# A hybrid decoder trunk on one core: the second stage with a Tanh for silu and inverse roots by Newton steps on GpSimd

## The chip, the cores and the metric

The kernel runs on one core of a Trainium2 chip. The metric is the device time of one execution in microseconds (us), the median of several runs. A core has five engines, each with its own instruction stream that it works off in order, and semaphores between them: TensorE (PE in the profile; its weight loads are listed as PEld), VectorE (DVE), ScalarE (ACT), GpSimd (POOL) and SyncE (SP), which here only issues DMAs.

## The reference, cut to what matters

The input is 2048 tokens of width 1024, ahead of which 16 "meta" tokens are set. Layer 0 is a gated DeltaNet with 8 heads of width 128: one projection to q, k, v and a gate z; a causal convolution of 4 taps and silu on q, k and v; k and q brought to unit length; then a chunked delta rule with a triangular system per chunk; a root-mean-square norm per head, times silu(z); an output projection. Layer 1 is sliding-window attention over a shared K/V, and a last norm follows. The change concerns layer 0 alone:

```python
def l2norm(x):
    return x * lax.rsqrt(jnp.sum(x * x, axis=-1, keepdims=True) + L2_EPS)

qkv = jax.nn.silu(causal_depthwise_conv(proj[..., :GDN_QKV_W], conv_w))
q = l2norm(qkv[..., :GDN_KEY_W].reshape(bsz, length, GDN_HEADS, GDN_DK)) * (GDN_DK ** -0.5)
k = l2norm(qkv[..., GDN_KEY_W:2 * GDN_KEY_W].reshape(bsz, length, GDN_HEADS, GDN_DK))
...
o = rmsnorm(o, o_norm) * jax.nn.silu(z.reshape(bsz, length, GDN_HEADS, GDN_DV))
```

## The kernel before

Four stages follow each other: norm and transposition of x, the DeltaNet (`gated_deltanet`, "second stage" here), its output projection with the shared K/V, and attention. The second stage works on 32 items: 4 groups of 512 tokens times 8 heads. The first 8 items (the head group) also carry a pass of their own for the 16 meta tokens, and in them the weights come in raw and are split in two parts (ScalarE rounds, GpSimd subtracts: `split_high`, `split_low`); later items load the parts.

An item goes through three steps of a pipeline, so step `it` has in hand item `it` (called p: projection, convolution, keys), item `it-1` (a: queries, the inverse of the triangular matrix X by levels) and item `it-2` (b: the scan over 4 chunks, norm, closing product). What lies where is written out by hand in `schedule`: 24 slots, each with its stages and with a number of projection matmuls (`FILL`) which TensorE works off after the slot's stages. Tables place the taps of the convolution (`TAPS`), the passes of the sigmoid (`SIGMOID`), silu (`SILU`), the copying of projections out of PSUM (`EVACUATE`), the splitting of weights (`SPLIT`) and the rows of the small triangular solve (`ROWS_P`, `ROWS_A`). Every engine runs through the same slots and does its own part; semaphores join them. Feature blocks are numbered f = 0 to 3 for k, v, q and z.

The lines that matter here, by the profile's numbers:

- L854 copies half a projection out of PSUM (ScalarE). L979 and L981 are the taps (VectorE), L983 a clamp at -40. L862, L865 and L868 are Exp, Ln and Exp of the sigmoid (ScalarE); L1002 and L1003 multiply silu out on VectorE, L1170 and L1171 on GpSimd (q and z in the head group).
- L1247 transposes kT (stage tokK, slot 12); L883 squares keys with a sum; L889, L894 and L895 (stage kk, slot 14) make 1/|k|^2 and |k| by Ln and Exp.
- L1050, L1052 and L1058 are VectorE's stage low (slot 15): the factors and the matrix nU. L1189 and L1194 are GpSimd's kg and qd, L1178 its part of splitting the weights, L843 ScalarE's.
- L1291, L1295 (left), L1308, L1311 (right), L1300 and L907 are the levels of the inverse (slots 13 to 18); between them VectorE writes half (L1083, L1087), X (L1095) and Xt (L1098).
- L1333 (ks), L1106 (r), L1342 (wr), L910 (w), L1347 and L1349 (out), L1111 (state) are the scan. L1116, L921, L922 and L926 are the output's norm, L1354 its transposes and L1125 the closing product (stage close, slot 16; slot 2 for a meta pass).
- L1023 and L1025 are the rows of the triangular solve.

Of the kernel before, what the change touches and what calls it, by code (L numbers as in the profile page):

```python
# [8 lines left out]
P = 128  # L9
# [3 lines left out]
META = 16  # L13
# [362 lines left out]
def gated_deltanet(nc, w_a, conv, o_gain, consts, table, xT_d, xg, oT_d, oTm_d, rows_d, rows_m_d, low_d, inv_d, w_d, w_out_next, w_raw):  # L376
# [6 lines left out]
    with nc.cleanup_on_exit(), ExitStack() as ctx:  # L383
# [18 lines left out]
        cst = sb("p2_cst", [P, 1])  # L402
# [8 lines left out]
        lnk = sb("p2_lnk", [P, 2, TPG])  # L411
# [28 lines left out]
        o_of = lambda p, c: ps_o1[:, P:2 * P] if p.meta else ps_o[c % 2][:, c * P:(c + 1) * P]  # L440
        ps_close = lambda p: ps_o1 if p.meta else ps_o0
# [20 lines left out]
        sig_done = sem("p2_sig_done")  # L462
# [8 lines left out]
        norm_ready = sem("p2_norm_ready")  # L471
        er_ready = sem("p2_er_ready")
# [35 lines left out]
        act_chain = sem("p2_act_chain")  # L508
# [28 lines left out]
        class Slot:  # L537
# [22 lines left out]
        def schedule(it, p, a, b, splitting):  # L560
# [17 lines left out]
            if b:  # L578
                if b[0].meta:
# [3 lines left out]
                    put(2, "close", b[0], 0)  # L583
                    put(4, "store", b[0], 0)
# [4 lines left out]
                put(16, "close", main, 0)  # L589
                put(18, "store", main, 0)  # L590
# [16 lines left out]
            if p:  # L607
# [6 lines left out]
                for q in p:  # L614
                    put(10, "gates", q, 0)
# [13 lines left out]
            for s, (back, f, parts) in SIGMOID.items():  # L629
                base[s].sigmoid += [(it - back, f, n) for n in parts if item[back]]  # L630
# [2061 lines left out]
```

## Time and profile before

| what | value |
| --- | --- |
| median of 3 runs | 2732.87 us (2731.5 to 2733.49) |
| the profiled execution | 2739.68 us |
| its span | 2737.9 us |
| busy: PE, DVE, ACT, POOL | 91%, 61%, 41%, 17% |
| second stage, first to last transposes of kT | 152.04 to 1493.14 us |
| mean granted TensorE clock | 0.961 |

The profile gives each instruction's start and duration, and for an engine's idle time what ended it. Overlapped matmuls make a busy TensorE look fuller than its peak. The span is the trace's own length; the execution's time is 1.8 us over it and 6.8 us over the median.

### The profile page before, as it was taken

How to read it: one execution, taken by the hardware profiler on the slowest of the kernel's cores; microseconds unless marked ns; L12 is line 12 of the kernel's file. 1: busy time of each engine (PE TensorE's matmuls, PEld its weight loads, DVE VectorE, ACT ScalarE, POOL GpSimd, SP SyncE). 2: the span in 40 equal slices, each digit the busy share in tenths (PEclk: the TensorE clock that was granted, in tenths of full speed). 3: DMA queues.
4: the chain of work that ended last, by engine and by line, in shares of the span. 5: the costliest groups of instructions: out<-in, count | busy, mean ns of one | idle time of the engine just before them, and what ended most of it. 6: DMA issues, size and time to landing. Idle time of an engine off the chain costs nothing. (4 is left out here: it accounts for less than half of the span.)

```text
span 2737.9 us, 46422 instructions
## 1 busy us (share of the span) xinstructions
PE 2485.1 (91%) x17193; PEld 2188.9 (80%) x17193; DVE 1672.3 (61%) x3906; ACT 1128.2 (41%) x3326; POOL 453.5 (17%) x341
## 2 busy tenths in 40 slices
PE   5468888899999999999999789999998999999997
PEld 4468777789998999999999558878886777777775
DVE  4357777777777777777777332233333667666764
ACT  4244554544444444444444244423332333333332
POOL 0033343310000000000000011200000333223331
PEclk9789999999999999999999589999999999999998
DMA  6664454544445444444453067743456322222221
GB/s 193 201 252 151 140 173 154 180 135 131 148 140 191 145 134 138 141 150 132 133 174 105 17 195 252 257 169 143 161 197 232 127 70 87 87 71 78 70 71 49
DMA packets 273665, 395.36 MB, mean 144 GB/s; under 512 B 79394, under 2 KB 187506, under 8 KB 273042
## 3 DMA queue, kind: packets, MB, share of 16 engines
q1 hardware_dynamic: 240642, 371.25, 40.5%
q10 hardware_dynamic: 32800, 21.17, 2.6%
q8 instruction: 136, 2.23, 0.3%
q14 instruction: 87, 0.71, 0.1%
HBM read 268.95 MB, written 123.95 MB: 144 GB/s over the span
## 5 line engine op out<-in xcount | busy, mean ns | idle before, releaser
L1229 PE MATMUL p_psp<-xg,p_whi 128*128 128x264 f32 x4096 | 842.6, 295 | 27.5 <-POOL p_wlo L1178 17.4
L1229 PEld LDWEIGHTS p_psp<-xg,p_whi 128*128 128x128 f32 x4096 | 655.1, 191 | 31.8 <-issue 29.4
L1229 PE MATMUL p_psp<-xg,p_wlo 128*128 128x264 f32 x2048 | 606.1, 296 | 0.0
L1229 PEld LDWEIGHTS p_psp<-xg,p_wlo 128*128 128x128 f32 x2048 | 391.5, 191 | 0.0
L981 DVE SCALAR_TENSOR_TENSOR p_acc<-p_proj,p_taps,p_acc 128x528 f32<-128x528 f32 x288 | 244.8, 850 | 4.6
L1854 PE MATMUL first_q<-first_w,p_o 128*128 128x512 f32 (+1 forms) x864 | 208.3, 400 | 15.7 <-DVE first_w L1818 15.7
L1854 PEld LDWEIGHTS first_q<-first_w,p_o 128*128 128x128 f32 (+1 forms) x864 | 157.1, 184 | 60.2 <-issue 16.0
L2400 PE MATMUL first_q<-first_w,p_hT 128*128 128x512 f32 x720 | 193.5, 408 | 11.6 <-DMA p_hT<-hT_dram 11.3
L2400 PE MATMUL p_pso<-p_wo,p_oT 128*128 128x512 f32 x768 | 193.9, 403 | 7.9 <-DVE p_oT L2311 4.2
L862 ACT ACTIVATE p_sig<-p_sig 128x528 f32<-128x528 f32 x128 | 82.6, 645 | 282.2 <-DVE p_sig L983 282.2
L1854 PE MATMUL p_psz<-p_wk,p_o 128*128 128x512 f32 x768 | 181.3, 392 | 0.0
L2400 PEld LDWEIGHTS p_pso<-p_wo,p_oT 128*128 128x128 f32 x768 | 143.6, 192 | 43.2 <-issue 10.4
L1023 DVE TENSOR_TENSOR p_prod<-p_Xb,p_blk 32x4 f32<-32x4 f32 (+13 forms) x448 | 163.8, 366 | 6.8
L1854 PEld LDWEIGHTS p_psz<-p_wk,p_o 128*128 128x128 f32 x768 | 142.9, 188 | 29.1
L2400 PEld LDWEIGHTS first_q<-first_w,p_hT 128*128 128x128 f32 x720 | 128.3, 189 | 46.3 <-DMA p_hT<-hT_dram 11.7
L1178 POOL TENSOR_TENSOR p_wlo<-raw,p_whi 128x512 fp32r<-128x512 f32 x72 | 106.3, 1486 | 274.4 <-ACT p_whi L843 274.2
L2151 ACT ACTIVATE p_logits<-p_logits,p_top 128x144 f32<-128x144 f32 x256 | 102.7, 403 | 81.5 <-DVE p_top L2253 81.5
L1189 POOL TENSOR_TENSOR p_kg<-p_kT,p_er 128x512 f32<-128x512 f32 (+1 forms) x40 | 45.2, 1129 | 543.3 <-ACT p_er L879 542.9
L2380 POOL TENSOR_TENSOR p_swapped<-p_q,p_cs 128x256 f32<-128x256 f32 x31 | 36.9, 1191 | 583.1 <-DVE p_q L2272 374.9
L854 ACT ACTIVATE p_proj<-p_psp 128x264 f32<-128x264 f32 x256 | 98.8, 386 | 62.7 <-PE p_psp L1229 62.5
L1194 POOL TENSOR_TENSOR p_qd<-p_qT,p_er 128x512 f32<-128x512 f32 (+1 forms) x40 | 50.7, 1275 | 429.2 <-DVE p_qT L1003 429.2
L907 ACT ACTIVATE p_Xt<-p_pst 128x512 f32<-128x512 f32 x64 | 38.3, 598 | 186.7 <-PE p_pst L1300 186.7
(264 smaller groups left out, 4711.5 us busy)
## 6 DMA issues: line engine op xcount, KB each, us to landing
p_whi<-w_dram SPq DMA_DIRECT2D x92, 512.0 KB, 3.9
p_wlo<-w_dram SPq DMA_DIRECT2D x92, 512.0 KB, 4.9
raw<-w_a_in SPq DMA_DIRECT2D x36, 512.0 KB, 6.8
w_dram<-p_whi SPq DMA_DIRECT2D x34, 512.0 KB, 4.4
w_dram<-p_wlo SPq DMA_DIRECT2D x34, 512.0 KB, 5.3
p_o<-hT_dram SPq DMA_DIRECT2D x34, 512.0 KB, 4.8
hT_dram<-p_hT SPq DMA_DIRECT2D x32, 512.0 KB, 3.4
p_hT<-hT_dram SPq DMA_DIRECT2D x30, 512.0 KB, 4.4
```

Source lines behind the costliest of these rows:

```text
L854: nc.scalar.activation(proj[:, f % 2, 3 + half_ * HALF:3 + (half_ + 1) * HALF], ps_p[half_][:, 0:HALF], ACT.Copy).then_inc(proj_read, 1)
L862: ins = nc.scalar.activation(v, v, ACT.Exp, scale=-1.0)
L907: nc.scalar.activation(Xt[p.par][:, 0:TPG, :], chunks(ps_t), ACT.Copy).then_inc(xt_ready, 1)
L981: nc.vector.scalar_tensor_tensor(a, p[:, part:part + GW], w, a, ALU.mult, ALU.add).then_inc(tap_done, 1)
L1023: link(nc.vector.tensor_tensor(t3, x3[:, 0:i, 0:i].rearrange("p j c -> p c j"), b3[:, 0:i, i].unsqueeze(1).to_broadcast([rows, i, i]), ALU ...
L1178: nc.gpsimd.tensor_tensor(w_lo[:, f, cols], w_raw[:, f % 2, cols], w_hi[:, f, cols].bitcast(f32), ALU.subtract).then_inc(lo_ready, 1)
L1189: nc.gpsimd.tensor_tensor(kg[p.par][:, at, :], cols(kT), e_r[:, at, :], ALU.mult).then_inc(keys_grown, 1)
L1194: nc.gpsimd.tensor_tensor(qd[p.par][:, at, :], cols(qT), e_r[:, at, :], ALU.mult).then_inc(queries_grown, 1)
L1229: ins = nc.tensor.matmul(ps_p[half_][:, 0:HALF], (w_hi, w_lo)[i][:, f, kc * P:(kc + 1) * P], xg[:, g % 2, j, kc, half_ * HALF:(half_ + 1) ...
L1854: last = nc.tensor.matmul(out, stationary[i][:, kc, 0:rows], moving(j, kc), start=kc == 0 and n == 0, stop=kc == KC - 1 and n == 2)
L2151: last_ = nc.scalar.activation(logits[:, s_, :], logits[:, s_, :], ACT.Exp, bias=top[:, s_:s_ + 1], accum_out=den[:, s_:s_ + 1])
L2400: ins = nc.tensor.matmul(banks[b][:], stationary[i][:, kc, :], weights[j][:, kc, b * FB:(b + 1) * FB], start=kc == 0 and n == 0, stop=kc = ...
```

## The change

1. silu(x) becomes (tanh(x/2) + 1) * x, which is twice silu. One Tanh on ScalarE replaces Exp, Ln and Exp, the clamp goes, and VectorE multiplies in one operation for all f (GpSimd's part goes). The factors of 2 are taken out later (0.25 on the sums of squares, half the output gain). The activation table is the one that has Exp and Tanh.
2. 1/|k|^2 comes from VectorE's reciprocal in stage low; |k| and the output's 1/sqrt come from GpSimd: a seed by integer arithmetic on VectorE, then three Newton steps of four small operations, each waiting for the one before it (stages root_k in slot 18; root_o in slot 16, and slot 1 for a meta pass). Two small buffers, `root[:, 0]` and `root[:, 1]`, hold minus half, the value and a temporary.
3. The output's scaling, transposes, closing product and store move: from slots 12, 16 and 18 to 18, 20 and 22, for a meta pass from 0, 2 and 4 to 4, 6 and 8. Meta outputs and their transposes lie in ps_t, the bank of the inverse's transposes, instead of ps_o1; a TensorE wait in ks goes, and two others come.

```diff
+TANH_EXP = "exp_and_others"
+ROOT_SEED = 0x5F3759DF
+ROOT_STEPS = 3
...
-        o_of = lambda p, c: ps_o1[:, P:2 * P] if p.meta else ps_o[c % 2][:, c * P:(c + 1) * P]
-        ps_close = lambda p: ps_o1 if p.meta else ps_o0
+        o_of = lambda p, c: ps_t[:, 0:P] if p.meta else ps_o[c % 2][:, c * P:(c + 1) * P]
+        ps_close = lambda p: ps_t[:, P:2 * P] if p.meta else ps_o0
...
-        SILU = {11: (0, 0), 21: (0, 1), 0: (1, 2), 5: (1, 3)}
+        TANH = {9: (0, 0), 19: (0, 1), 22: (0, 2), 1: (1, 3)}
+        SILU = {10: (0, 0), 20: (0, 1), 23: (0, 2), 3: (1, 3)}
...
-                    put(2, "close", b[0], 0)
-                    put(4, "store", b[0], 0)
+                    put(1, "root_o", b[0], 0)
+                    put(4, "scale", b[0], 0)
+                    put(6, "close", b[0], 0)
+                    put(8, "store", b[0], 0)
...
-                put(16, "close", main, 0)
-                put(18, "store", main, 0)
+                put(20, "close", main, 0)
+                put(22, "store", main, 0)
...
+                for q in p:
+                    put(18, "root_k", q, 0)
...
+                put(16, "root_o", b[-1], 0)
+                put(18, "scale", b[-1], 0)
...
-                elif stage == "kk":
-                    l = lnk[:, p.which, 0:n]
-                    act.wait_ge(k_squared, k + 1)
-                    link(nc.scalar.activation(l, ssq[:, p.which, 0, 0:n], ACT.Ln, bias=cst[:]))
...
-                    nc.scalar.activation(rn2[:, p.which, 0:n], l, ACT.Exp, scale=-1.0).then_inc(norm_ready, 1)
-                    nc.scalar.activation(norm[:, p.which, 0:n], l, ACT.Exp, scale=0.5).then_inc(norm_ready, 1)
...
                 elif stage == "low":
+                    squared = n2[:, p.which, 0:n]
                     nc.vector.tensor_copy(e_last[par][:, p.which, 0:n], mine[:, 4, 0:n])
-                    dve.wait_ge(norm_ready, 2 * k + 1)
-                    nc.vector.scalar_tensor_tensor(nD[par][:, p.which, 0:n], rn2[:, p.which, 0:n], -1.0,
+                    link(nc.vector.tensor_scalar(squared, ssq[:, p.which, 0, 0:n], 0.25, L2_EPS, ALU.mult, ALU.add))
+                    link(nc.vector.reciprocal(rn2[:, p.which, 0:n], squared))
+                    nc.vector.scalar_tensor_tensor(nD[par][:, p.which, 0:n], rn2[:, p.which, 0:n], -0.25,
...
                     last.then_inc(low_ready, 1)
+                    if not zero(k):
+                        dve.wait_ge(norm_ready, k)
+                    if not zero(p.first):
+                        dve.wait_ge(vs_ready, p.first)
+                    link(nc.vector.tensor_scalar(root[:, 0, 0, 0:n], squared, -0.5, None, ALU.mult))
+                    nc.vector.tensor_scalar(root[:, 0, 1, 0:n].bitcast(i32), squared.bitcast(i32), -0.5, float(ROOT_SEED),
+                                            ALU.mult, ALU.add).then_inc(norm_seeded, 1)
...
+            def inverse_root(kind, n, last=None):
+
+                minus_half, y, t = (root[:, kind, x, 0:n] for x in range(3))
+                for turn in range(ROOT_STEPS):
+                    link(nc.gpsimd.tensor_tensor(t, y, y, ALU.mult))
+                    link(nc.gpsimd.tensor_tensor(t, t, minus_half, ALU.mult))
+                    link(nc.gpsimd.tensor_scalar(t, t, 1.5, None, ALU.add))
+                    step_done = nc.gpsimd.tensor_tensor(y, y, t, ALU.mult)
...
+                elif stage == "root_k":
+                    pool.wait_ge(norm_seeded, k + 1)
+                    y = inverse_root(0, p.n)
+                    nc.gpsimd.tensor_tensor(norm[:, p.which, 0:p.n], n2[:, p.which, 0:p.n], y, ALU.mult).then_inc(norm_ready, 1)
+                elif stage == "root_o":
+                    pool.wait_ge(ms_seeded, k + 1)
+                    inverse_root(1, p.n, last=ms_ready)
...
-                        if index == 1 and p.with_meta:
-                            pe.wait_ge(o_g_ready, k)
```

In the instruction lists, VectorE's stage low of the main pass in a head item reads as follows before the change (p_rn is rn2, p_psl the bank of the inverse's products, p_cur the pass's decays; a semaphore whose name begins with p1_ is one of this stage that has taken over a number of the first):

```order
L1050 COPY p_elast<-p_cur 128x4
L1052 SCALAR_TENSOR_TENSOR p_nD<-p_rn,p_cur 128x4 [waits p2_norm_ready]
L1058 SCALAR_TENSOR_TENSOR p_nU<-p_psc,p_nD,p_eg 128x128 [waits p2_decay_ready,p2_kk_ps,p2_scaled]
L1058 SCALAR_TENSOR_TENSOR p_nU<-p_psc,p_nD,p_eg 128x128 x3
L1125 SCALAR_TENSOR_TENSOR p_og<-p_pso,p_gain,p_zT 128x512 [waits p2_stored,p1_a_exp,p2_oT_ps]
L1095 TENSOR_TENSOR p_X<-p_X,p_psl 128x8x32 [waits p2_right_ps]
```

And with the change (p_n is n2, the sum of squares):

```order
L1034 COPY p_elast<-p_cur 128x4
L1035 TENSOR_SCALAR p_n<-p_ssq 128x4
L1036 RECIPROCAL p_rn<-p_n 128x4 [waits p2_dve_chain]
L1037 SCALAR_TENSOR_TENSOR p_nD<-p_rn,p_cur 128x4 [waits p2_dve_chain]
L1043 SCALAR_TENSOR_TENSOR p_nU<-p_psc,p_nD,p_eg 128x128 [waits p2_decay_ready,p2_kk_ps,p2_scaled]
L1043 SCALAR_TENSOR_TENSOR p_nU<-p_psc,p_nD,p_eg 128x128 x3
L1051 TENSOR_SCALAR p_root<-p_n 128x4 [waits p2_vs_ready,p2_norm_ready]
L1052 TENSOR_SCALAR p_root<-p_n 128x4 [waits p2_dve_chain]
L1087 TENSOR_TENSOR p_X<-p_X,p_psl 128x8x32 [waits p2_right_ps]
```

The closing product has left this place, four small operations have come, and the wait on norm_ready stands behind nU, ahead of the addition into X.

GpSimd in a head item before the change, from the kg products on (p_wlo are the weights' low parts):

```order
L1189 TENSOR_TENSOR p_kg<-p_kT,p_er 128x128 [waits p2_ks_ps,p1_a_exp,p2_er_ready]
L1189 TENSOR_TENSOR p_kg<-p_kT,p_er 128x512 [waits p1_a_exp,p2_er_ready]
L1178 TENSOR_TENSOR p_wlo<-raw,p_whi 128x512 [waits p1_cum_read] x4
L1170 TENSOR_TENSOR p_qT<-p_acc,p_sig 128x16 [waits p2_kq_ps,p2_queries_grown,p1_a_exp,p1_raw_in]
L1171 TENSOR_TENSOR p_qT<-p_acc,p_sig 128x512
```

And with the change, up to the first turn of the output's root:

```order
L1184 TENSOR_TENSOR p_kg<-p_kT,p_er 128x128 [waits p2_ks_ps,p1_a_exp,p2_er_ready]
L1184 TENSOR_TENSOR p_kg<-p_kT,p_er 128x512 [waits p1_a_exp,p2_er_ready]
L1173 TENSOR_TENSOR p_wlo<-raw,p_whi 128x512 [waits p1_cum_read] x2
L1159 TENSOR_TENSOR p_root<-p_root 128x4 [waits p2_ms_seeded]
L1160 TENSOR_TENSOR p_root<-p_root 128x4 [waits p2_pool_chain]
L1161 TENSOR_SCALAR p_root<-p_root 128x4 [waits p2_pool_chain]
L1162 TENSOR_TENSOR p_root<-p_root 128x4 [waits p2_pool_chain]
```

These four rows come three times; then the root of the meta key (128x1, with L1188 at its end, which signals norm_ready), then that of the main key (128x4). Only after these 38 steps come the other two of the four subtractions.

VectorE behind the inverse, from the row that gives the state's first value, with the change:

```order
L1068 MEMSET p_state 128x128
L1120 SCALAR_TENSOR_TENSOR p_og<-p_pso,p_gain,p_zT 128x512 [waits p2_stored,p1_a_exp,p2_oT_ps]
L984 SCALAR_TENSOR_TENSOR p_vT<-p_sig,p_acc 128x16 [waits p2_v_ps,p1_raw_in]
L986 SCALAR_TENSOR_TENSOR p_vT<-p_sig,p_acc 128x512
L961 TENSOR_SCALAR p_acc<-p_proj,p_taps 128x528 [waits p1_a_exp,p1_rows_ready]
L964 SCALAR_TENSOR_TENSOR p_acc<-p_proj,p_taps,p_acc 128x528 [waits p1_act_chain]
```

The closing product (L1120) and silu of v now stand ahead of the taps of q; before, the taps and the first rows of the solve stood ahead of silu of v.

## Rows read from the trace of the kernel before

**Rows 1.** The page, part 1: busy us, share of the span and count by engine.
```profile
PE 2485.1 (91%) x17193; PEld 2188.9 (80%) x17193; DVE 1672.3 (61%) x3906; ACT 1128.2 (41%) x3326; POOL 453.5 (17%) x341
```

**Rows 2.** Timeline of TensorE: start us, us, line, instruction [idle before, released by]; slot 12.
```profile
152.04 0.47 PE L1247 MATMUL p_psk<-p_ident,p_kT 128*128 128x128 f32 x1 [9.23 <-DVE p_kT L1003]
...
200.00 0.33 PE L1247 MATMUL p_psk<-p_ident,p_kT 128*128 128x128 f32 x1 [4.11 <-DVE p_kT L1003]
...
353.24 0.33 PE L1247 MATMUL p_psk<-p_ident,p_kT 128*128 128x128 f32 x1 [0.34 <-DVE p_kT L1003]
...
643.14 0.66 PE L1247 MATMUL p_psk<-p_ident,p_kT 128*128 128x128 f32 x4 [0.53 <-DVE p_kT L1003]
```

**Rows 3.** Stretches: an ordinary and a head item: us, busy by engine, clock, DMA, GB/s.
```profile
643.14:683.32 40.18, 38.92 (x321) 37.55 (x321) 30.66 (x86) 18.80 (x61) 2.56 (x2) 1.00 0.45 143
353.24:403.97 50.73, 42.49 (x338) 39.84 (x338) 37.82 (x97) 26.05 (x85) 19.24 (x16) 1.00 0.49 163
```

**Rows 4.** Timeline of TensorE, the ordinary item: its wait for the state.
```profile
669.10 0.49 PE L1333 MATMUL p_psc<-p_state,p_kg 128*128 128x128 f32 x2 [0.38 <-DVE p_state L1111]
```

**Rows 5.** Timeline of TensorE, the head item from 353.24: its waits over one us.
```profile
377.34 0.46 PE L1342 MATMUL p_psc<-p_r,p_Xt 128*128 128x128 f32 x2 [1.81 <-DVE p_r L1106]
...
387.70 0.48 PE L1229 MATMUL p_psp<-xg,p_whi 128*128 128x264 f32 x2 [1.03 <-ACT p_proj L854]
...
401.95 0.49 PE L1347 MATMUL p_psc<-p_w,p_kdec 128*128 128x128 f32 x2 [1.12 <-ACT p_w L910]
```

**Rows 6.** Timeline of VectorE, the same item, slots 15 to 21.
```profile
361.80 1.13 DVE L1058 SCALAR_TENSOR_TENSOR p_nU<-p_psc,p_nD,p_eg 128x128 f32<-128x128 f32 x4
362.84 0.74 DVE L1125 SCALAR_TENSOR_TENSOR p_og<-p_pso,p_gain,p_zT 128x512 f32<-128x512 f32 x1
363.50 0.41 DVE L1095 TENSOR_TENSOR p_X<-p_X,p_psl 128x256 f32<-128x256 f32 x1
...
368.28 0.41 DVE L983 TENSOR_SCALAR p_sig<-p_acc 128x528 f32<-128x528 f32 x1
...
370.81 0.18 DVE L1002 TENSOR_TENSOR p_vT<-p_acc,p_sig 128x16 f32<-128x16 f32 x1 [0.49 <-ACT p_sig L868]
370.90 0.69 DVE L1003 TENSOR_TENSOR p_vT<-p_acc,p_sig 128x512 f32<-128x512 f32 x1
```

**Rows 7.** Timeline of GpSimd, the same item: the subtraction of slot 15.
```profile
362.71 1.28 POOL L1178 TENSOR_TENSOR p_wlo<-raw,p_whi 128x512 fp32r<-128x512 f32 x1 [1.04 <-ACT p_whi L843]
```

**Rows 8.** Timeline of ScalarE, the same item, slot 15.
```profile
361.73 0.39 ACT L854 ACTIVATE p_proj<-p_psp 128x264 f32<-128x264 f32 x1
362.00 0.63 ACT L843 ACTIVATE p_whi<-raw 128x512 fp32r<-128x512 f32 x1
```

**Rows 9.** Groups of instructions of GpSimd, shapes apart: count | busy us, mean ns | idle before.
```profile
L1189 POOL TENSOR_TENSOR p_kg<-p_kT,p_er 128x128 f32<-128x128 f32 x8 | 3.7, 460 | 67.1 <-ACT p_er L879 67.1
L1170 POOL TENSOR_TENSOR p_zT<-p_proj,p_sig 128x16 f32<-128x16 f32 x7 | 1.5, 218 | 49.3 <-ACT p_sig L868 49.3
L2678 POOL MEMSET const-bfloat16-1.0<- 128x1 bf16 x1 | 0.1, 101 | 0.0
```

**Rows 10.** The same view: an operation (attention stage) that waits for GpSimd's operation before.
```profile
L2384 POOL TENSOR_TENSOR p_q<-p_q,p_cs 128x512 f32<-128x512 f32 x31 | 40.4, 1303 | 2.4
```

**Rows 11.** Groups of instructions of ScalarE: the second pass of the sigmoid.
```profile
L865 ACT ACTIVATE p_sig<-p_sig 128x528 f32<-128x528 f32 x128 | 82.9, 648 | 1.3
```

**Rows 12.** Stretches after TensorE's idle time, columns as above: the clock is third from last.
```profile
200.00:204.00 4.00, 4.00 (x21) 4.00 (x22) 0.86 (x4) 1.85 (x12) 0.00 (x0) 0.57 0.97 386
...
888.20:897.30 9.10, 8.70 (x47) 8.49 (x48) 3.69 (x11) 1.01 (x5) 1.28 (x1) 0.62 0.76 228
```

**Rows 13.** Timeline of TensorE, an ordinary item: the output's four transposes (slot 16).
```profile
851.12 0.60 PE L1354 MATMUL p_pso<-p_ident,p_on 128*128 128x128 f32 x4
```

**Rows 14.** Timeline of VectorE and of GpSimd, the head item: two operations at once.
```profile
387.82 1.12 DVE L1023 TENSOR_TENSOR p_prod<-p_Xb,p_blk 40x169 f32<-40x169 f32 x1
...
387.53 1.09 POOL L1171 TENSOR_TENSOR p_zT<-p_proj,p_sig 128x512 f32<-128x512 f32 x1
```

More of the change, by code:

```diff
@@ L410, in gated_deltanet @@
         ssq = sb("p2_ssq", [P, 2, 2, TPG])
-        lnk = sb("p2_lnk", [P, 2, TPG])
+        n2 = sb("p2_n2", [P, 2, TPG])
+        root = sb("p2_root", [P, 2, 3, TPG])
         norm = sb("p2_norm", [P, 2, TPG])
@@ L628, in schedule @@
                 base[s].taps += [(it - back, f, n) for n in parts if item[back]]
-            for s, (back, f, parts) in SIGMOID.items():
-                base[s].sigmoid += [(it - back, f, n) for n in parts if item[back]]
+            for s, (back, f) in TANH.items():
+                base[s].tanh += [(it - back, f)] if item[back] else []
             for s, (back, f) in SILU.items():
@@ L942, in step @@
                         evacuate(item, u)
-                    for item, f, part in slot.sigmoid:
-                        sigmoid(item, f, part)
+                    for item, f in slot.tanh:
+                        half_angle_tanh(item, f)
                     for item, f, part in slot.split:
                         split_high(item, f, part)
-            nc.scalar.preload_act_table_set(LN_EXP)
+            nc.scalar.preload_act_table_set(TANH_EXP)
             act.wait_ge(const_in, 16 * N_CONST)
@@ L966, in convolve @@
             def convolve(it, f, part):
-                p, a, v = proj[:, f % 2, :], acc[:, f % 2, :], sig[:, f % 2, :]
-                w = taps[:, 4 * f + part:4 * f + part + 1] if part < 4 else None
-                if part == 0 or f == 3:
+                p, a = proj[:, f % 2, :], acc[:, f % 2, :]
+                w = taps[:, 4 * f + part:4 * f + part + 1]
+                if part == 0:
                     dve.wait_ge(proj_read, 2 * NF * it + (2 * f + 2))
@@ L1134, in step @@
                     for q, item, f in slot.silu:
-                        if f < 2 or not splitting[1]:
-                            silu(q, item, f, b)
+                        silu(q, item, f, b)
                     for item, f, part in slot.taps:
@@ L1140, in step @@
                         solve_row(q, i)
-            nc.vector.memset(cst[:], L2_EPS)
             nc.vector.memset(proj[:, :, 0:3], 0.0)
@@ L1148, in _ @@
             dve.wait_ge(const_in, 16 * N_CONST)
+            link(nc.vector.tensor_scalar(gain[:], gain[:], 0.5, None, ALU.mult))
             dve.wait_ge(zeroed, 32)
@@ L1200, in step @@
                         stage_of(stage, q, index, b)
-                    for q, item, f in slot.silu:
-                        if f >= 2 and splitting[1]:
-                            silu(q, item, f, b)
                     for item, f, part in slot.split:
@@ L1298, in stage_of @@
                     if index:
+                        if index == 1 and b and b[0].meta:
+                            pe.wait_ge(o_g_ready, b[0].number + 1)
                         for c in range(n):
@@ L1320, in stage_of @@
                         pe.wait_ge(qk_ready, k + 1)
+                        if p.meta and a and a[0].meta:
+                            pe.wait_ge(vs_ready, a[0].number + 1)
                         if p.leading:
```

125 lines of the change are left out of this document (51 added, 74 removed).

## Prediction, made before the change was run

> **What bounds the kernel now.** I began with the page's busy times: TensorE is at work 91% of the span [rows 1], so a change pays only where TensorE waits. The diff stays inside the second stage, so I then listed TensorE's starts of one instruction that comes once a pass, the transposes of kT that open slot 12 [rows 2]. They divide the stage into items, and the table of stretches gives an item's length and TensorE's busy time in it [rows 3]: 38.92 us of 40.18 in an ordinary item, but 42.49 of 50.73 in one of the head group (items 0 to 7, each with its meta pass). An ordinary item can therefore give at most 1.26 us (24 items: 30 us) and a head item 8.24 us (8 items: 66 us). More can't be won, since TensorE's instructions stay what they are; what can be lost has no such limit.
>
> The waits say what the change can reach. In the ordinary item the larger two are 0.53 us for kT and 0.38 for the state [rows 2, 4]. In the head item the reader should see two kinds [rows 5]: ScalarE is late (1.03 us for a copied projection, 1.12 us for w) because it stands in the three passes of the old sigmoid, and VectorE is late (1.81 us for r).
>
> **The one place that decides: a wait put on VectorE.** The change keeps the seeds of all key roots in one small buffer, root[:, 0]. So before it writes the seeds of a pass, stage "low" waits until the root of the pass before is finished (norm_ready of at least k). In an ordinary item that was done long before. In a head item the pass before is the meta pass of the same item, and GpSimd computes that root only in slot 18, behind the two kg products, two subtractions of weights (slots 14 and 15) and, from item 2 on, the output's root (slot 16). VectorE comes to the wait in slot 15 and works strictly in order: the addition into X (L1095), on which TensorE's next step of the inverse (L1295) waits, stands right behind it.
>
> Worked out on the head item from 353.24: VectorE ends the products of "low" at 362.93 [rows 6]. GpSimd's second subtraction starts at 362.71, released by ScalarE, and takes 1.28 us: GpSimd is free at 363.99 [rows 7]. That moment stays, since ScalarE's copy at 362.00, on which it waits, stands behind the copy of a projection at 361.73, which TensorE sets [rows 8]. Then come 12 chained steps of the output's root and 13 of the meta key's.
>
> A chained GpSimd step of 1 or 4 columns has no row. The nearest are 0.218 us at 16 columns and 0.460 at 128, so 2.2 ns a column over about 0.19 [rows 9]; and where a GpSimd operation waits for the one before it, the idle time is 2.4 us over 31, 0.08 us each [rows 10]. I take 0.27 us. Bounds: 0.10 (a memset of one column, without a hand-over) and 0.54 (128 columns with it).
>
> 25 steps of 0.27 are 6.75 us: GpSimd is done at 370.74. Two small VectorE operations (0.18 each, as the 16-column one) and the addition of 0.41 follow: X is there at 371.51 instead of 363.91 [rows 6]. **TensorE stands 7.6 us longer per head item**, six times (items 2 to 7): 45.6 us. With 0.10 it would be 3.4 us, with 0.54 14.4. Item 1 has no output behind it, 12 steps less: 4.3 us. In item 0 no inverse is open, so TensorE waits for no X: 0. Sum **+50 us**.
>
> **The other terms.**
> - VectorE's crowded part, from slot 20 to slot 12, gets the closing product of the output (0.66 us until the next start) and, from GpSimd, silu of q (0.18 + 0.69, as vT's now), and loses two clamps of 0.41 [rows 6]: 0.7 us more before the first r, which is late already. With 0.3 for the moved transposes it is 1.0. GpSimd's root of the meta output falls beside later rows of the inverse: 0. Seven items: **+7 us**.
> - ScalarE loses two of three sigmoid passes, each 0.65 us [rows 11], four times an item. In head items this frees the waits of 1.03 and 1.12 us, of which I give 0.55 back to VectorE, the next one late. Seven times 1.6: **-11 us**. In ordinary items these passes lie beside TensorE's projections, which don't wait for them: 0.
> - TensorE's clock. After 4.11 us of idle time [rows 2] the next 4.00 us ran at a granted 0.57; one stretch of 9.10 us after another wait ran at 0.62 [rows 12]. Most of these is 1.2 instead of 2.4 GHz, worth 4.00 x 0.43 = 1.7 and 9.10 x 0.38 = 3.5 us. The new stall of 7.6 us, and the one before r, will do this too: 3 us in six items, **+18 us** (bounds 0 and 7 each).
> - Ordinary items. silu of k ends a slot earlier: -0.53. The closing transposes leave slot 16 for 20, so TensorE is there sooner at L1295; but X is not, for "low" gets four small operations (0.18 each) before the addition and loses only the 0.66 of the closing product [rows 6]: +0.4. Before the first r VectorE is some 1.1 us later (closing product and silu of q, less a clamp), TensorE only by the transposes (0.60 [rows 13]): +0.5 against the 0.38 that the state costs there today. Together 0 (bounds -0.9 and +0.5), 24 times: **0**. GpSimd's 25 steps lie between slots 14 and 20, beside a VectorE that mostly reads PSUM: 0; without that cover up to 0.2 us a step.
> - Start and end. Silu of k in items 0 and 1, for which TensorE waits 9.23 and 4.11 us [rows 2], is two ScalarE passes and a clamp shorter: -3 us. At the very end nothing hides the output's root, 12 x 0.27: +3 us. Together **0**.
> - SP's queue and the other stages move only with these shifts. The meta outputs' new bank takes away a TensorE wait on o_g_ready that shows no idle time in [rows 5]: 0.
>
> Sum: 50 + 7 - 11 + 18 = **+64 us**. The profiled execution took 2739.68 us, 1.8 over its span and 6.8 over the median of the three runs. Set on the median, the forecast is 2732.87 + 64 = **2797 us**.
>
> **A rule weighed.** A VectorE product with both operands in SBUF does not run beside a GpSimd operation here: started at 387.82, it ended at 388.94, 0.32 us after GpSimd's at 387.53 + 1.09 [rows 14]. The Trainium skill ("SBUF — State Buffer", section "SBUF: two separate sides") says that the two engines share one pair of ports as an exclusive lock, and that whoever comes second waits for the whole of the other's instruction. By that rule small work moved to GpSimd slows VectorE down; the trace agrees. My sum holds it at 0, for VectorE stands still during most of the new steps; the first rival prices it.
>
> **Rivals.**
> 1. *The lock decides* (0.10). Of the 50 GpSimd steps of a head item, the 25 that are not run while VectorE is held meet its rows and taps and hold it up by 0.2 us each [rows 9, 14]. For it: VectorE is the late engine in the crowded part, and the main key's root runs there. Against it: by my times most of that root is done before. 25 x 0.2 = 5 us in 7 items: 2797 + 35 = 2832 us.
> 2. *Faster: the shortened engines win* (0.07). Place: the two waits for ScalarE and that for kT in a head item (1.03, 1.12, 0.34 [rows 2, 5]) and the two in an ordinary one (0.53, 0.38). All gone, and no block: 7 x 2.5 + 24 x 0.9 = 39 us, 2694 us. It decides only if GpSimd has the meta root done when VectorE arrives, at 362.9; but the second subtraction starts only then, and 25 steps follow. Even at 0.10 us a step it comes 3.6 us too late.
> 3. *No change* (0.03). The block costs 3.4 us in six items and 2.1 in the seventh (0.10 a step), no clock falls, and ordinary items gain 0.9: 22 + 7 - 11 - 22 = -4 us, 2729 us.
>
> **How the numbers follow.** The forecast has 0.80. Its own bounds: at 0.10 us a step the block is 28 us less, the clock perhaps 8 less, ordinary items 10 less: 2751 us. At 0.54 it is 44 us more: 2841 us. The range 2751 to 2841 takes in rival 1 and leaves out rivals 2 and 3 and the forecast's tails. Differences under 0.2% (5.5 us) can't be told from none by a measurement of this kernel. Slower: the forecast and rival 1, 0.90; same 0.03; faster 0.07.
>
> **What would show it.** In a head item VectorE idle for 7 to 9 us, released by GpSimd, before the two small writes into p_root that follow the four products into p_nU; TensorE idle as long before the half-width step of the inverse, its clock lower right after; head items of 58 to 63 us. GpSimd's steps 0.25 to 0.3 us apart. TensorE's waits for a copied projection and for w gone there. Ordinary items of 39.3 to 40.8 us, without a wait for kT. The forecast is wrong if that idle time of VectorE is under 3 us, if the steps are far from 0.27 us, or if ordinary items move by over 1 us.

## The result and the profile after

The changed kernel takes **2809.05 us** (median of 4 runs, 2806.42 to 2815.97) against 2733.18 us of the kernel before in the same series: ratio 1.0266, 95% interval [1.0253, 1.0279], slower. The forecast was 2797 us (2751 to 2841). The profiled execution took 2806.55 us (span 2804.8), 66.9 us more than the profiled one before. That difference is what the traces can explain; the medians differ by 76 us because the execution profiled before lay 6.8 us above the median it was shown with, and the one after 2.5 below its own.

The page, part 1, busy us by engine, answers [rows 1]: ScalarE lost about a sixth of its work, GpSimd got 972 more instructions, TensorE has the same number and is busy 21.9 us longer.

```profile
PE 2507.0 (89%) x17193; PEld 2216.3 (79%) x17193; DVE 1666.6 (59%) x4046; ACT 953.0 (34%) x2870; POOL 684.7 (24%) x1313
```

Stretches of an ordinary and of a head item, to be held against [rows 3] (kT's transposes are L1248 now; these are later in the span, but the same kinds of item):

```profile
795.91:835.47 39.56, 38.71 (x323) 37.53 (x322) 30.32 (x87) 13.64 (x49) 9.58 (x27) 1.00 0.45 141
380.71:442.70 61.99, 46.80 (x338) 44.30 (x339) 39.09 (x110) 19.80 (x67) 26.32 (x62) 0.86 0.38 129
```

The ordinary item is 0.62 us shorter, the head item 11.26 us longer: 6.95 of it idle time of TensorE, and 4.31 us in which its 338 matmuls simply took longer, at a mean granted clock of 0.86.

TensorE in the head item, its waits over 0.3 us from the start to the scan (those of before are [rows 2, 5] and the two rows behind these):

```profile
380.71 0.33 PE L1248 MATMUL p_psk<-p_ident,p_kT 128*128 128x128 f32 x1 [0.87 <-DVE p_kT L986]
...
399.06 1.33 PE L1296 MATMUL p_psl<-p_X,p_nU 64*128 64x64 f32 x5 [8.02 <-DVE p_X L1087]
...
407.86 0.33 PE L1267 MATMUL p_pst<-p_ident,p_vT 128*128 128x128 f32 x1 [0.30 <-DVE p_vT L986]
...
413.01 0.46 PE L1336 MATMUL p_psc<-p_state,p_kg 128*128 128x128 f32 x2 [2.19 <-DVE p_vs L1057]
...
416.12 0.77 PE L1345 MATMUL p_psc<-p_r,p_Xt 128*128 128x128 f32 x2 [1.94 <-DVE p_r L1098]
```

And two rows of TensorE in the head item of the kernel before. The wait of 1.54 us for v belongs to the waits over one us, but [rows 5] and the prediction leave it out.

```profile
363.96 1.10 PE L1295 MATMUL p_psl<-p_X,p_nU 64*128 64x64 f32 x8 [0.33 <-DVE p_X L1095]
...
371.64 0.33 PE L1266 MATMUL p_pst<-p_ident,p_vT 128*128 128x128 f32 x1 [1.54 <-DVE p_vT L1003]
```

Of the 8.02 us for X all but 0.33 is new. So is the wait for the meta v (p_vs), which the text of the prediction did not name. VectorE at the same place: its products into nU end at 390.45, then it stands until GpSimd's L1188 has written the meta norm; the addition into X is third in line.

```profile
389.26 1.19 DVE L1043 SCALAR_TENSOR_TENSOR p_nU<-p_psc,p_nD,p_eg 128x128 f32<-128x128 f32 x4
398.31 0.17 DVE L1051 TENSOR_SCALAR p_root<-p_n 128x4 f32<-128x4 f32 x1 [7.86 <-POOL p_norm L1188]
398.52 0.17 DVE L1052 TENSOR_SCALAR p_root<-p_n 128x4 int32<-128x4 int32 x1
398.60 0.41 DVE L1087 TENSOR_TENSOR p_X<-p_X,p_psl 128x256 f32<-128x256 f32 x1
```

And GpSimd: the second subtraction, the first of 12 steps for the output, the first of 13 for the meta key, and the last.

```profile
390.16 1.28 POOL L1173 TENSOR_TENSOR p_wlo<-raw,p_whi 128x512 fp32r<-128x512 f32 x1 [2.41 <-ACT p_whi L846]
391.39 0.20 POOL L1159 TENSOR_TENSOR p_root<-p_root 128x4 f32<-128x4 f32 x1
...
394.73 0.19 POOL L1159 TENSOR_TENSOR p_root<-p_root 128x1 f32<-128x1 f32 x1
...
398.09 0.19 POOL L1188 TENSOR_TENSOR p_norm<-p_n,p_root 128x1 f32<-128x1 f32 x1
```

From 391.39 to 398.28 are 25 chained steps: 0.276 us each. Finally the clock at and behind the two pauses, third column from the end (1.00 is 2.4 GHz, 0.50 is 1.2 GHz); in [rows 3] the whole item ran at 1.00:

```profile
396.71:400.71 4.00, 1.65 (x8) 1.65 (x8) 1.34 (x4) 0.00 (x0) 2.69 (x12) 0.50 0.80 280
400.71:404.71 4.00, 4.00 (x23) 3.53 (x23) 1.10 (x3) 1.91 (x6) 1.64 (x8) 0.56 0.00 0
412.71:416.71 4.00, 1.76 (x11) 1.60 (x12) 2.92 (x9) 0.44 (x1) 1.28 (x1) 0.72 0.37 148
416.71:420.71 4.00, 4.00 (x20) 4.00 (x20) 1.49 (x8) 1.02 (x4) 0.71 (x4) 0.50 0.72 249
```

Taken over the second stage, from one start of the transposes to the next: items 2 to 7 together 65.8 us longer (306.72 to 372.52), item 1 5.55, item 8 3.06, items 9 to 30 together 7.7 shorter, start and end +0.2. That is the 66.9 us.

### The profile page after: what moved, and what is told of

The parts are those of the page before. It is cut to its first block and busy times, and to the rows that moved or that the text cites. A ratio compares the mean times of both kernels' runs of the same rounds, so it can differ in the third digit from the quotient of the medians.

```text
span 2804.8 us, 47209 instructions
## 1 busy us (share of the span) xinstructions
PE 2507.0 (89%) x17193; PEld 2216.3 (79%) x17193; DVE 1666.6 (59%) x4046; ACT 953.0 (34%) x2870; POOL 684.7 (24%) x1313
## 5 line engine op out<-in xcount | busy, mean ns | idle before, releaser
L1230 PE MATMUL p_psp<-xg,p_whi 128*128 128x264 f32 x4096 | 859.3, 299 | 20.6 <-POOL p_wlo L1173 17.4
L1230 PEld LDWEIGHTS p_psp<-xg,p_whi 128*128 128x128 f32 x4096 | 667.7, 195 | 24.1 <-issue 21.4
L1230 PE MATMUL p_psp<-xg,p_wlo 128*128 128x264 f32 x2048 | 613.6, 300 | 0.0
L1230 PEld LDWEIGHTS p_psp<-xg,p_wlo 128*128 128x128 f32 x2048 | 397.6, 194 | 0.0
L1006 DVE TENSOR_TENSOR p_prod<-p_Xb,p_blk 32x4 f32<-32x4 f32 (+13 forms) x448 | 150.8, 337 | 7.6
L902 ACT ACTIVATE p_w<-p_psc,p_nD 128x128 f32<-128x128 f32 x136 | 50.0, 367 | 198.5 <-PE p_psc L1345 197.8
L1008 DVE TENSOR_REDUCE p_Xb<-p_prod 32x2 f32<-32x4 f32 (+13 forms) x448 | 105.0, 234 | 15.4
```

The costliest lines, as they stand in the source:

```text
L902: nc.scalar.activation(w_sb[:], ps_c[:, P:2 * P], ACT.Copy, scale=nD[p.par][:, p.which, index:index + 1]).then_inc(w_ready, 1)
L1006: link(nc.vector.tensor_tensor(t3, x3[:, 0:i, 0:i].rearrange("p j c -> p c j"), b3[:, 0:i, i].unsqueeze(1).to_broadcast([rows, i, i]), ALU ...
L1008: link(nc.vector.tensor_reduce(x3[:, i, 0:i], t3, mybir.AxisListType.X, ALU.add))
L1230: ins = nc.tensor.matmul(ps_p[half_][:, 0:HALF], (w_hi, w_lo)[i][:, f, kc * P:(kc + 1) * P], xg[:, g % 2, j, kc, half_ * HALF:(half_ + 1) ...
```

## The experiments

Every run is set against runs of the kernel before on the same chip in the same series; their medians stood at 2733 to 2739 us. "Head" is the mean of items 2 to 7, "ordinary" one undisturbed item of the main group, both from the starts of kT's transposes.

| run | median us | ratio to before, 95% | head | ordinary |
| --- | --- | --- | --- | --- |
| before | | 1 | 51.1 | 40.18 |
| the change | 2809.05 | 1.0266 [1.0253, 1.0279] | 62.1 | 39.56 |
| two_sets | 2756.97 | 1.0078 [1.0061, 1.0094] | 54.4 | 39.57 |
| steps5 | 2844.25 | 1.0392 [1.0374, 1.0409] | 67.0 | 39.55 |
| vs_early | 2808.13 | 1.0259 [1.0241, 1.0276] | 62.2 | 39.57 |
| two_sets_vs | 2756.51 | 1.0066 [1.0049, 1.0083] | 54.6 | 39.57 |
| meta_root_early | 2764.59 | 1.0088 [1.0070, 1.0105] | 55.9 | 39.57 |
| two_sets_q0 | 2742.21 | 1.0002 [0.9985, 1.0020] | 54.4 | 39.26 |
| early_q0 | 2752.07 | 1.0054 [1.0038, 1.0071] | 54.3 | 39.31 |
| early_q0_steps2 | 2742.69 | 1.0016 [1.0007, 1.0026] | 53.4 | 39.27 |
| all_moves | 2734.41 | 0.9985 [0.9976, 0.9994] | 53.9 | 39.00 |
| all_moves_steps2 | 2715.08 | 0.9915 [0.9899, 0.9931] | 50.6 | 39.00 |
| k_silu11 | 2812.83 | 1.0273 [1.0257, 1.0289] | 62.1 | 39.62 |
| root_slot15 | 2732.24 | 0.9974 [0.9962, 0.9986] | 53.5 | 38.99 |

**Is it the shared buffer? (two_sets)** The two keys' roots get a buffer each, and the wait goes back to the item before.

```diff
-        root = sb("p2_root", [P, 2, 3, TPG])
+        root = sb("p2_root", [P, 3, 3, TPG])
...
-                    if not zero(k):
-                        dve.wait_ge(norm_ready, k)
                     if not zero(p.first):
+                        dve.wait_ge(norm_ready, p.first)
                         dve.wait_ge(vs_ready, p.first)
-                    link(nc.vector.tensor_scalar(root[:, 0, 0, 0:n], squared, -0.5, None, ALU.mult))
+                    link(nc.vector.tensor_scalar(root[:, p.which, 0, 0:n], squared, -0.5, None, ALU.mult))
...
```

> One edit: the seeds and steps of the meta key's root and of the main key's root get a buffer each, so stage low no longer waits for the root of the pass before. Theory A (VectorE's wait for the shared buffer is the loss): the 8.0 us of idle time in items 2 to 7 and about 4.3 in item 1 go, with 1 to 3 us of half clock behind each: 52 to 70 us less than the change, 2740 to 2757 us; head items of 51 to 54 us instead of 62 to 63; ordinary items as in the change (39.55). Theory B (the steps on GpSimd themselves hold VectorE up, by the port they share, wherever they lie): VectorE goes on but its products beside the 25 steps get 0.2 us longer each and TensorE then waits at r: at most 3 of the 8 us come back per item, 2785 to 2795 us.

51 of the 73 us above before went (2.66% to 0.78% of 2737): theory A, at the slow edge of its range (the head items, 54.4 us, just outside it). TensorE's wait for X fell from 8.02 to 0.98 us. What is left of it has another cause: VectorE's first seed write, 0.17 us in the change, took 1.06 us beside GpSimd's subtraction and ended 0.03 us behind it, and the addition into X stands behind it (timelines of VectorE and of GpSimd, two_sets):

```profile
370.78 1.06 DVE L1050 TENSOR_SCALAR p_root<-p_n 128x4 f32<-128x4 f32 x1
...
370.54 1.27 POOL L1172 TENSOR_TENSOR p_wlo<-raw,p_whi 128x512 fp32r<-128x512 f32 x1 [2.35 <-ACT p_whi L846]
```

Two more things are left in the head item. First the waits ahead of the scan, by the timeline of TensorE:

```profile
384.68 0.46 PE L1335 MATMUL p_psc<-p_state,p_kg 128*128 128x128 f32 x2 [1.32 <-DVE p_vs L1056]
...
389.57 0.77 PE L1344 MATMUL p_psc<-p_r,p_Xt 128*128 128x128 f32 x2 [3.72 <-DVE p_r L1097]
```

and then the clock, by the table of stretches: the item, and the stretches behind the pause at X and behind the pause at r.

```profile
361.09:415.64 54.55, 45.54 (x339) 43.01 (x340) 39.91 (x110) 19.91 (x67) 29.29 (x62) 0.91 0.44 150
373.09:377.09 4.00, 4.00 (x24) 3.53 (x24) 0.85 (x3) 1.94 (x6) 2.94 (x15) 0.57 0.38 122
389.09:393.09 4.00, 3.52 (x16) 3.55 (x17) 1.08 (x5) 1.02 (x4) 0.00 (x0) 0.50 0.91 339
```

TensorE's idle time is 9.01 us, only 0.77 over the 8.24 of [rows 3]; its busy time is 45.54, 3.05 over. So of the 3.8 us that this item still lacks, 3.05 are TensorE's busy time, at a mean granted clock of 0.91. Why r comes late: VectorE first waits 0.89 us for the main key's root, and then the 36-column row of the solve lasts 1.27 us where it took 0.20 (at 415.06) in the change. The 16-column operation ahead of it, silu of q, lasts 0.50 us; here the change was no better (0.64 at 413.90, it too beside a subtraction), while the same line took 0.17 for v at 407.03. Timeline of VectorE, two_sets:

```profile
385.81 0.69 DVE L1056 TENSOR_TENSOR p_vs<-p_psk,p_norm 128x512 f32<-128x512 f32 x1 [0.89 <-POOL p_norm L1187]
386.42 0.50 DVE L984 SCALAR_TENSOR_TENSOR p_qT<-p_sig,p_acc 128x16 f32<-128x16 f32 x1
386.84 0.68 DVE L986 SCALAR_TENSOR_TENSOR p_qT<-p_sig,p_acc 128x512 f32<-128x512 f32 x1
387.45 1.27 DVE L1006 TENSOR_TENSOR p_prod<-p_Xb,p_blk 40x36 f32<-40x36 f32 x1
```

GpSimd's two subtractions ran beside them: by GpSimd's timeline (next row) the first ended at 386.89, and the pair at 388.64, 0.08 us before the 36-column row of the solve.

```profile
385.63 1.26 POOL L1172 TENSOR_TENSOR p_wlo<-raw,p_whi 128x512 fp32r<-128x512 f32 x1
```

This is the behaviour of [rows 14] at another place. The rule cited in the prediction (the Trainium skill, "SBUF — State Buffer", "SBUF: two separate sides": an exclusive lock for the whole instruction) fits both rows: each VectorE operation ends just behind GpSimd's.

**A dose of steps (steps5).** `ROOT_STEPS = 3` becomes 5.

> One number: five Newton steps instead of three in every root. Theory A: in items 2 to 7 sixteen more chained operations lie ahead of VectorE's seeds (eight of the output's root, eight of the meta key's), in item 1 eight: 16 x 0.28 = 4.5 us x 6 + 2.2 = 29 us, with a little half clock and 2 us at the very end: 2838 to 2850 us, head items of 66 to 68 us, ordinary items within 0.2 us of 39.55, since there the steps lie beside other work. Theory B: every added step costs VectorE 0.2 us also in ordinary items (16 more steps there, 3.2 us x 24 = 77): 2900 us or more, ordinary items of 41 us or more.

Timeline of TensorE, the corresponding item:

```profile
420.15 1.96 PE L1296 MATMUL p_psl<-p_X,p_nU 64*128 64x64 f32 x8 [12.52 <-DVE p_X L1087]
```

12.52 - 8.02 = 4.50 us for 16 more steps, 0.281 each; head items +4.9, ordinary ones unchanged, the time as theory A had it. The waits behind the block are those of the change: 0.31, 2.19 and 1.94 us for v, the meta v and r. Theory B (every step costs VectorE something) falls for the ordinary items, and the head item's waits don't show it either.

**Is the wait for the meta v a loss of its own? (vs_early, two_sets_vs)**

```diff
-                    insert(22, ("tokV", p[0], 0), ("vs", p[0], 0))
+                    insert(21, ("tokV", p[0], 0), ("vs", p[0], 0))
```

> One edit: the transposes and the scaling of the meta v (tokV and vs of the meta pass) come one slot earlier, ahead of the last taps of q and one row of the solve on VectorE. In the change TensorE stands 2.19 us in a head item for the meta v before the scan's first product, a wait that the change brought in when the meta outputs went into the bank of the meta v's transposes. Theory A2 (that wait is lost time): 1.5 to 2.2 us x 7 less, 2792 to 2800 us, with r's wait behind it not longer. Rival (VectorE's backlog is the limit there, whatever stands first): what is won at the meta v is lost again at r, which stands behind the same rows and taps: 2804 to 2812 us.

> Both edits, separate buffers and the meta v one slot earlier. If both theories hold the gains add up: 2725 to 2742 us, near the kernel before, with head items of 49 to 52 us. If only the shared buffer counts: the time of the run with that edit alone, within 4 us.

No, twice. The 2.19 us went and came back at r, by the timeline of TensorE in vs_early:

```profile
420.68 0.77 PE L1345 MATMUL p_psc<-p_r,p_Xt 128*128 128x128 f32 x2 [3.97 <-DVE p_r L1098]
```

2.19 + 1.94 = 4.13 in the change, 3.97 here, and the wait for v ahead of them rose from 0.30 to 0.93 us. The wait is VectorE's backlog, met at whichever semaphore comes first; the change added a name, not a cost.

**The place instead of the buffer (meta_root_early).** The shared buffer stays; the meta key's root runs right after its seeds.

```diff
-                    insert(12, ("low", p[0], 0))
+                    insert(12, ("low", p[0], 0), ("root_k", p[0], 0))
...
-                for q in p:
-                    put(18, "root_k", q, 0)
+                put(18, "root_k", main, 0)
```

> One edit, the shared buffer stays: the meta key's root runs on GpSimd right after its seeds, ahead of the kg products, the subtractions and the output's root. Theory A (the loss is the place of that root behind other GpSimd work, not the buffer): VectorE's 8.0 us go as with separate buffers, 2757 us or less; and since the main key's root then ends 13 x 0.28 = 3.6 us sooner than with separate buffers, VectorE's wait of 0.89 us for it ahead of the main v goes too: 2744 to 2756 us, head items of 52 to 54.5 us. Rival: the 13 steps delay the kg products and the subtractions, and with them the weights, and TensorE waits for those instead: 2765 us or more.

Between the two, and nearer to the rival: the block is gone without a second buffer, but the median is 8 us over that of two_sets, outside theory A's range, and the head items of the traces are 1.5 us longer (the intervals of the two against the kernel before overlap). The 13 steps now push the kg products and the subtractions later, and what waits is not the weights but X again: two operations of VectorE's stage low last 0.90 and 1.16 us beside the subtractions, as shown for all_moves below. Timeline of TensorE:

```profile
375.84 1.68 PE L1295 MATMUL p_psl<-p_X,p_nU 64*128 64x64 f32 x8 [2.22 <-DVE p_X L1086]
```

**Silu of q behind r (two_sets_q0).** `SILU` has `0: (1, 2)` in place of `23: (0, 2)`.

> Separate buffers, and silu of q goes from slot 23 to slot 0 of the next step, behind the first r, where it was before the change (but still on VectorE). With separate buffers alone TensorE waits 3.72 us for r in a head item, and VectorE's two operations for q (0.50 + 0.68, the first held by GpSimd's subtraction) lie ahead of r. Theory C1 (VectorE's count of work ahead of r is the limit): r comes 1.1 us sooner in 7 items, and 0.28 in 24 ordinary ones: 14 us less, 2740 to 2746 us. Theory C2 (GpSimd's subtractions hold VectorE's row of the solve to their own end, whatever lies ahead of it: the row took 1.27 us instead of 0.20 and ended 0.08 us after them): in head items under 0.4 us, so 5 to 9 us less in all, 2748 to 2753 us, with the row's operation then 2 us or longer.

The time is C1's (15 us less, level with before), but not by C1's account, as far as the trace shows. It is of an execution of 2747.35 us, 5 over the median, and 8 us below the one profiled of two_sets. Items 9 to 30 give 6.4 of that, 0.31 us each in the undisturbed ones; where the rest of the 15 us comes from no trace shows. In the head item r's wait did fall by 1.2 us (3.72 to 2.51), yet the item stayed at 54.58, by its stretches:

```profile
360.47:415.05 54.58, 46.74 (x339) 44.22 (x340) 40.22 (x110) 19.92 (x67) 29.21 (x62) 0.91 0.44 148
372.47:376.47 4.00, 4.00 (x22) 3.53 (x22) 0.51 (x2) 1.94 (x6) 2.86 (x16) 0.50 0.39 124
376.47:380.47 4.00, 4.00 (x24) 4.00 (x25) 1.77 (x4) 0.86 (x3) 3.09 (x13) 0.67 0.80 280
```

Idle time went down to 7.84 us, below the 8.24 of before, and busy time up by 1.20: the stretch at the lower clock behind the pause at X (0.99 us) is longer here, 0.50 and 0.67 where two_sets had 0.57 and 1.00. In this execution, what had been won in waiting was lost in the clock.

**Both, and fewer steps (early_q0, early_q0_steps2).**

> The early meta root and silu of q in slot 0 together. If both add: 2757 less 6 for VectorE's wait for the key's root less 14 for r: 2730 to 2742 us, no slower than the kernel before; head items of 50.5 to 52.5 us, ordinary items of 39.2 to 39.4. If GpSimd's subtractions decide when r comes: 2742 to 2752 us.

> The same with two Newton steps instead of three (a relative error of some 5 in a million in the roots). If the block is gone, the steps lie beside other work and their count no longer matters: within 3 us of the run with three steps, of which 1 us is the output's root at the very end. If GpSimd still sets when VectorE goes on: 4 to 10 us less.

The time, 2752 us, is the second range's upper edge. Silu of q gave 12.5 us against meta_root_early, near its 14; what did not come is the gain of the early root, whose wait for X is still 2.21 us in this trace. With two steps the time was 9 us less and that wait 1.00 us: GpSimd still set VectorE's pace.

**Four moves (all_moves, all_moves_steps2).** To early_q0 come the main key's seeds behind the addition into X (a stage "seed" in slot 17) and the closing product in slot 19:

```diff
-                put(20, "close", main, 0)
-                put(22, "store", main, 0)
+                put(19, "close", main, 0)
+                put(21, "store", main, 0)
...
+                put(17, "seed", main, 0)
...
```

> Four moves and the shared buffer: the meta key's root early, silu of q in slot 0, the main key's seeds in slot 17 (behind the addition into X instead of ahead of it), the closing product in slot 19 instead of 20, so that VectorE doesn't stand for TensorE's transposes. Against the run with the first two moves: TensorE's 2.2 us for X fall to 0.6 and with them a stretch at half clock (1.7 us), VectorE is 1.5 us sooner at the meta v and at r: 3 to 4.5 us in 7 items, 21 to 31 us: 2716 to 2731 us if TensorE's two pauses and the clock behind them are all that is left of the loss; head items of 49.5 to 51.5 us. Rival: the pause ahead of the scan stays (VectorE's rows of the solve are held by GpSimd's subtractions) and the half clock with it: head items of 52 to 53 us, 2733 to 2745 us.

> The same with two Newton steps: if GpSimd's chain is now off every path, within 2 us of the run with three; if it still sets VectorE's pace, 4 to 10 us less.

With three steps 2734 us: the rival. With two steps 2715 us, **0.85% faster than the kernel before** and the best version of this study; my expectation that the count might no longer matter was wrong by 19 us, and the other one, 4 to 10 us, was too small. In the trace with three steps, VectorE's timeline in stage low:

```profile
366.57 0.90 DVE L1045 COPY p_elast<-p_cur 128x4 f32<-128x4 f32 x1
367.39 0.16 DVE L1046 TENSOR_SCALAR p_n<-p_ssq 128x4 f32<-128x4 f32 x1
367.58 0.18 DVE L1047 RECIPROCAL p_rn<-p_n 128x4 f32<-128x4 f32 x1
367.79 1.17 DVE L1048 SCALAR_TENSOR_TENSOR p_nD<-p_rn,p_cur 128x4 f32<-128x4 f32 x1
```

beside GpSimd's two subtractions, by its timeline:

```profile
365.70 1.75 POOL L1181 TENSOR_TENSOR p_wlo<-raw,p_whi 128x512 fp32r<-128x512 f32 x1
367.67 1.27 POOL L1181 TENSOR_TENSOR p_wlo<-raw,p_whi 128x512 fp32r<-128x512 f32 x1 [0.22 <-ACT p_whi L846]
```

Operations of 4 columns ended at 367.47 and 368.96, GpSimd's at 367.45 and 368.94. TensorE then waited 1.93 us for X. With four steps fewer ahead of it the first subtraction ended at 355.14, before stage low began at 355.97, and the wait was, in the timeline of TensorE with two steps,

```profile
358.21 1.10 PE L1304 MATMUL p_psl<-p_X,p_nU 64*128 64x64 f32 x8 [0.38 <-DVE p_X L1095]
```

The items of the two kernels follow: 54.56 us (busy 46.44) and 51.13 (busy 44.78).

**Place or number? (root_slot15)** Three steps, the meta key's root between the two subtractions:

```diff
-                    insert(12, ("low", p[0], 0), ("root_k", p[0], 0))
+                    insert(12, ("low", p[0], 0))
+                    put(15, "root_k", p[0], 0)
```

> The four moves with three Newton steps, but the meta key's root in slot 15, between GpSimd's two subtractions, instead of ahead of the kg products. In the four moves together that root pushed the first subtraction to 365.70 (1.75 us) and the second to 367.67 (1.27 us), and three small operations of VectorE's stage low took 0.90, 1.17 and 0.34 us beside them instead of 0.15, 0.16 and 0.3, so that TensorE waited 1.93 us for X. Theory D (GpSimd's long subtractions hold VectorE's small operations where they meet; their place decides, not the number of Newton steps): now only short root steps lie beside stage low, TensorE's wait for X falls under 0.8 us, no half clock follows, head items of 50.5 to 52 us as with two steps: 2712 to 2724 us, faster than the kernel before by 0.4% or more. Rival (the number of steps itself matters: the chain of 38 sets VectorE's pace wherever it lies): head items of 53 us or more, 2729 to 2738 us.

Theory D was right on X (no wait over 0.25 us is left there) and wrong on the time, which lies in the rival's range. The rest of the chain is now late for the output: ScalarE waits 4.33 us for the output's root, and TensorE for ScalarE (its timeline):

```profile
375.13 1.12 PE L1366 MATMUL p_pso<-p_ident,p_on 128*128 128x128 f32 x4 [3.57 <-ACT p_on L916]
```

In the three places tried for the meta key's root, 38 chained steps of 0.28 us (10.6 us) and the four subtractions of a head item always met something that waits. The best time with three steps is this one, 0.26% under the kernel before; two steps in the earlier place gave 0.85%. Two steps in this place, and separate buffers together with the four moves, were not run.

**Where the ordinary item's 0.62 us come from (k_silu11).** The change with `SILU` 10 back at 11.

> The change with one move undone: silu of k in slot 11 again instead of 10. The change's ordinary items are 0.62 us shorter than before's (39.56 against 40.18). If that comes from silu of k alone, they go back to 40.1 to 40.2 and TensorE's wait of 0.5 us for kT returns: 22 items x 0.6 = 13 us more than the change, 2820 to 2826 us; if it comes from the shorter sigmoid, whose Tanh stays, 0 to 0.2 us an item: under 5 us more.

Ordinary items 39.62, 0.06 more: the slot is worth almost nothing. TensorE's wait for kT does not return; its timeline shows no idle time ahead of the transposes:

```profile
798.48 0.66 PE L1248 MATMUL p_psk<-p_ident,p_kT 128*128 128x128 f32 x4
```

So it was the shorter sigmoid that made silu of k early, not the table.

## Why the prediction was right

- **The block**, "TensorE stands 7.6 us longer per head item". 8.02 us, of which 0.33 were there before: 7.7. The step was put at 0.27 us and came as 0.276 and 0.281 (steps5); GpSimd's free moment, the second subtraction's end, stood where the text had it. two_sets took the wait away and 51 us with it. Shown.
- **"VectorE's crowded part", +1.0 an item.** The waits for v, the meta v and r together went from 1.54 + 1.81 = 3.35 to 0.30 + 2.19 + 1.94 = 4.43 us: +1.1. The size was right, though set against too small a start, for the 1.54 us at v were overlooked. The place was not: about half of the 4.43 us shows at the new wait for the meta v, which my text passed over in "the meta outputs' new bank ... 0". vs_early shows that this wait costs nothing of its own.
- **ScalarE, "-1.6".** The waits for the copied projection and for w are gone, 1.03 + 1.12 = 2.15 us; the 0.55 held back for VectorE came back as 0.53 at kT (0.34 to 0.87 us). Net -1.6.
- **The clock, "3 us in six items": mis-sized.** 4.31 us in the item shown, from the busy time of the same 338 matmuls; by the stretches of all of them 24.6 us in items 2 to 7 instead of 18, and 2.2 in item 1, for which the sum had nothing. Both causes that the prediction names are there, the stall for X and the pause ahead of the scan, each with a stretch at 1.2 GHz behind it; their size was too small.
- **"Ordinary items ... 0": mis-sized, within its bounds.** -0.62 us in an undisturbed item; 17 of the items 9 to 30 are 0.47 to 0.67 us shorter, the other five are not (item 15 is 1.92 longer, its cause was not looked into), which leaves the 7.7 us. In the item from 795.91 the waits for kT (0.53) and for the state (0.38) went, one of 0.33 for r and one of 0.17 for Xt came: 0.41 less. The other 0.21 are TensorE's busy time, 38.92 to 38.71. The +0.4 for X did not come: in the item from 795.91 TensorE starts L1296 after 8.97 us, in the one from 723.48 it started L1295 after 9.04, neither with a wait. k_silu11 also corrects the reason given: not "silu of k ends a slot earlier", but fewer passes before it.
- **Start and end, 0**: -1.9 and +2.1 us.
- **Not in the sum**: item 8, which has no meta pass of its own but finishes those of others, +3.1 us. By its stretch 2.7 of that are TensorE's busy time (41.09 to 43.81 us), at a mean granted clock of 0.93 where the kernel before had 1.00; what made the clock fall there was not looked into.

The sum 50 + 7 - 11 + 18 = 64 stands against 71.4 in items 1 to 7, 3.1 in item 8, -7.7 in the ordinary ones and 0.2 at the ends: 67 us. In items 1 to 7 TensorE's idle time grew by 44.5 us, against 50 + 7 - 11 = 46, so the terms for the waits were right; its busy time grew by 26.9, against 18 for the clock. The two mis-sized terms (clock +9, ordinary items -8) cancel. That the sum comes within 3 us of the traces is thus in part luck. By the medians the change costs 76 us, and 2809 lies 12 over the forecast.

**The rivals.** *The lock decides*: not in the change (VectorE stands still during 25 of the steps, and with five Newton steps neither the ordinary items nor the head item's waits behind the block grow). But once the block is gone it is the next limit, and not by the small steps that the rival priced: it is the 1.3 us subtractions, pushed about by the steps, that hold VectorE's smallest operations. *Faster*: its condition, the meta root done when VectorE comes, had to be made by hand (two_sets), and even then the clock and the lock took the gain; the nearest to it, 2715 us against the rival's 2694, needed four moves and a Newton step less. *No change* falls with 0.28 us a step.

## What to carry to other kernels

Where an in-order engine is made to wait for a long chain of small operations on another, ask what stands right behind the wait: here two seed writes into a shared buffer of 12 columns held up an addition on the critical path, and a second buffer bought back 51 of 73 us. A chain moved to a quiet engine also moves that engine's long operations, and these may land beside the small ones of its neighbour. And a pause is to be priced with the clock behind it: compare TensorE's busy time for the same matmuls, not the waits alone.

## What the runs showed of the hardware that was not expected

- VectorE and GpSimd hold each other up in both directions, very small operations too, and on VectorE not only products of two operands: VectorE's copy of 4 columns took 0.90 us instead of 0.16 beside a GpSimd subtraction, and a GpSimd step of 4 columns 0.70 instead of 0.20 when it came 0.11 us behind one of VectorE's taps (the second row, of the changed kernel's GpSimd, against 398.93 + 0.76 of VectorE).

```profile
398.77 0.20 POOL L1159 TENSOR_TENSOR p_root<-p_root 128x4 f32<-128x4 f32 x1 [0.49 <-DVE p_root L1052]
399.04 0.70 POOL L1160 TENSOR_TENSOR p_root<-p_root 128x4 f32<-128x4 f32 x1
```

- A TensorE pause of about 1 us at X was followed by 1.2 GHz in two_sets (0.57 for 4 us) and two_sets_q0 (0.50, then 0.67); in the kernel before, the pauses of 1.54 and 1.81 us at v and at r were not (the whole item at 1.00). What tells them apart was not tried.
- Steps of 1 and of 4 columns on GpSimd cost the same (0.19 and 0.20 us, 0.28 from start to start): between these two widths only the number of steps counts.
